# Moving the early half of an expert scatter ahead of a branch, and weight splits to other places, in a two-block transformer kernel

## The chip, the core and the metric

The kernel runs on one core of one Trainium2 chip. The metric is the device time of one execution in microseconds (us): the median of several runs, each timed from the start of the program to its end.

## What is computed

The input is 256 tokens of 1024 features, in float32, and a second sequence of 256 memory tokens. Two blocks of two layers each follow one another. Cut to what matters here:

```
first block, layer 0:  x += gate * (concat(retention(h), chunk_attention(h)) @ even_w_out)
             layer 1:  x += gate * (stick_breaking(h) @ odd_w_out)
  after each of them:  x += gate * grouped_moe(h)
second block, layer 0: x += norm(fox_and_nsa(h) @ ev_w_out)
              layer 1: x += norm(differential(h) @ od_w_out)
  after each of them:  x += norm(softmax((h @ wq) k_mem^T / 8) v_mem @ wo)   # 4 heads of 64
                       x += norm((silu(h @ wg) * (h @ wu)) @ wd)             # swiglu, 2816 wide
```

`grouped_moe` has 16 experts in 4 groups. Each token picks one group and two experts in it. The modulation of the first block (`gate`, and the scales and shifts inside `h`) comes from a matrix `ada_w` that is applied to one conditioning vector.

## The kernel before

**Products.** A float32 product is made of three TensorE products of rounded parts: each operand is the sum of a high part and a low part, and the low-by-low product is left out (`products`, L815 to L817; in the swiglu L1710 and L1711). A feature that PE turns into a bank goes to ScalarE (ACT), which writes the high part, and then to VectorE (DVE), which subtracts it for the low part.

**Weights.** SP's queue loads weights into a ring of three tiles of 1 MB, each in two halves of 512 KB. ACT copies a half to its high part (L1801, the helper `splits`), DVE subtracts for the low part (L2445, its own `splits`), and PE multiplies. DVE's subtraction is also what frees the half of the ring for SP's next load (L632). Both split buffers hold three tiles: ACT splits tile s only after PE has used tile s-3. The order of splits on ACT and DVE relative to their other work is written out by hand: a call `splits(end)` goes on with whole tiles up to a number, and waits if the load has not landed.

**Experts.** `experts(l)` runs a loop of four passes. Pass p computes, for the p-th expert of each group, up to a fixed number of gathered tokens. Tokens beyond that number are handled by an overflow body behind `If(over == 1)`; with these inputs the body is not taken, and each engine jumps over it. After the branch, `scatter` adds each pass's rows back to their tokens, with 32 matmuls for each layer (L1272 and L1273): 12 for the first three passes and the first two column parts, which need only the passes before the last (`early`), and 20 more which need the last pass's output too (`late`).

**Attention a0.** The first layer's chunk attention takes its pairs of heads in steps t. In each step, ACT writes exponentials and copies turned probabilities (L2000) and outputs (L2004, features of the output projection); DVE subtracts row maxima, scales, and writes the low part of the output features (L2755). Slices of the `ada` product are woven in on PE. `HIGH_AHEAD` and `LOW_AHEAD` name the steps at which ACT and DVE split whole tiles of `even_w_out`. PE then waits for all attention features before it starts `project("even_out")`, whose first tile multiplies features of the retention alone.

**Memory cross attention.** `cross(l)` on ACT: take 8 features (`take_features`), split weight tiles (the third of them, called f0 here, is the first of the swiglu that follows, and the next is f1), take the memory's projection (`take_mem`), copy the projected queries (L1854, `take_chunks`), split f1, and run the attention with its exponentials. The table of the exponential is loaded on ACT at the first of them, and `warm(ACT.Sqrt)` loads the root's table after the attention (L1874). DVE splits all these tiles ahead of its part of the attention (`shift`, L2717). After the attention comes the output projection, whose squares (L1879) ACT makes and whose norm DVE applies.

**End of the first swiglu.** The state is turned in 16 units of 128 features by 128 tokens (PE L930, ACT `take_state` L1838, DVE `low_state` L2676), which PE fills with products of the next projection `od_in`. Two calls `add_rows` on DVE add the normed rows to x (L2634). ACT then makes squares of x and splits the first tile of `od_in`'s second column group; DVE follows.

Of the kernel before, what the change touches and what calls it, by code (L numbers as in the profile page):

```python
# [15 lines left out]
KD = D // 128  # L16
# [10 lines left out]
RING = 3  # L27
# [167 lines left out]
def build(nc, a, out):  # L195
# [3 lines left out]
    with ctx:  # L199
# [244 lines left out]
        HIGH_AHEAD, LOW_AHEAD = {"a0": (4, 5), "b0": ()}, {"a0": (4, 6), "b0": ()}  # L444
# [348 lines left out]
        def _(eng):  # L793
# [470 lines left out]
            def scatter(m, l, high, taken, sources):  # L1264
# [12 lines left out]
                early, late = sources[:-1], sources[-1:]  # L1277
                if early:
                    eng.wait_ge(m["y_taken"], taken - 1)
                    for c in range(2):  # L1280
                        add_part(c, early, opens=True)
# [64 lines left out]
            def experts(l):  # L1346
# [21 lines left out]
                with eng.If(over == 1):  # L1368
                    def wait_over(i):
                        eng.wait_ge(ovf_loaded[l][i % RING], 16 * (i // RING + 1))  # L1370
                        return slot(i), slot(i)
                    eng.wait_ge(moe["y_taken"], PASSES * (l + 1) + 1)
                    experts_pass(ovf[l], 0, 5 * l + 4, wait_over, True)
# [404 lines left out]
        def _(eng):  # L1778
# [11 lines left out]

            def splits(end):

                while at_split[0] < end:
                    s = at_split[0]
                    at_split[0] += 1
                    t = tiles[plan.splits[s]]
                    for i in range(2):
                        eng.wait_ge(w_loaded[t["slot"]][i], t["loaded"])
                        if s >= SPLITS and i == 0:
                            eng.wait_ge(weights_used, tiles[plan.splits[s - SPLITS]]["order"] + 1)  # L1800
                        eng.activation(half_of(high(s), i, t["size"]), half_of(slot(t["n"]), i, t["size"]), ACT.Copy)\  # L1801
                           .then_inc(high_ready, 1)
# [1863 lines left out]
```

## Time and profile before

| what | us |
|---|---|
| median of 3 runs | 1750.7 |
| lowest and highest of the 3 | 1748.95, 1750.95 |
| the profiled execution's own time | 1750.65 |
| span of the profiled execution | 1748.9 |
| TensorE busy in that span | 1657.4 |

The profile shows one execution. PE is TensorE, DVE VectorE, ACT ScalarE, POOL GpSimd, SP the engine that issues the loads. Every instruction has its start, its duration, and the idle time of its engine before it, with what ended that idle time in square brackets. PEclk is the granted clock of TensorE as a share of full speed: 1.00 is 2.4 GHz, 0.50 is 1.2 GHz. Matmuls are pipelined, so that the distance between two starts tells more than one duration.

### The profile page before, as it was taken

The numbers are of one execution on the slowest core, as the hardware profiler recorded it, in microseconds if no ns is written. First come the engines' busy times: TensorE is split into PE (matmuls) and PEld (weight loads), VectorE is DVE, ScalarE is ACT, GpSimd is POOL, SyncE is SP. The second block draws the span as 40 slices with busy tenths as digits, with TensorE's granted clock in tenths as the row PEclk, the third lists the DMA queues.
The fourth block names the chain that finished last, engine by engine and source line by source line (L and its number), as shares of the span: only waits on it lengthen the run. The fifth ranks groups of instructions, "written<-read, shape, count | busy, mean of one in ns | idle before, by whom it ended". The sixth has DMA issues, their size and how long they took to land.

```text
span 1748.9 us, 24863 instructions
## 1 busy us (share of the span) xinstructions
PE 1657.4 (95%) x8427; PEld 1338.7 (77%) x8427; DVE 1278.9 (73%) x2067; ACT 1096.5 (63%) x1693; POOL 13.1 (1%) x27
## 2 busy tenths in 40 slices
PE   5998999999989999999999898889999898989998
PEld 3775778888878768888888787678888676868886
DVE  3874598988977586989989766676666657666665
ACT  3545488888864464888888675665444647654443
POOL 1000000000000000000000000000000000000000
PEclk8999899999999998999999999999999999989999
DMA  9878489999977563999999663116555551325552
GB/s 357 314 270 331 181 322 322 388 331 347 369 273 257 200 216 122 338 327 383 329 339 379 213 217 145 49 73 217 191 170 199 176 193 49 144 88 183 188 192 72
DMA packets 113345, 413.36 MB, mean 236 GB/s; under 512 B 13024, under 2 KB 13072, under 8 KB 112880
## 3 DMA queue, kind: packets, MB, share of 16 engines
q1 hardware_dynamic: 110208, 400.74, 63.3%
q0 software_dynamic: 1936, 8.59, 1.5%
q10 hardware_dynamic: 1120, 2.99, 0.4%
q8 instruction: 47, 0.77, 0.2%
q14 instruction: 34, 0.28, 0.0%
HBM read 411.21 MB, written 1.05 MB: 236 GB/s over the span
## 4 chain that ended last, share of the span: by engine, by line
PE 75%; DVE 10%; ACT 7%; issue 4%; DMA 3%; DVEq 0%; SPq 0%; ACTq 0%
PE banks L815 16%; PE banks L817 15%; PE banks L816 15%; PE banks L1710 10%; PE banks L1711 5%; DVE weights_low L2445 4%; PE banks L1033 1%; ACT qk_features L2050 1%; PE banks L992 1%; PE banks L832 1%; DMA weight_ring<-in_ada_w 1%; PE banks L845 1%; ACT weights_high L2142 1%; ACT scratch L1988 1%; ACT weights_high L1801 1%
## 5 line engine op out<-in xcount | busy, mean ns | idle before, releaser
L2445 DVE TENSOR_TENSOR weights_low<-weight_ring,weights_high 128x1024 fp32r<-128x1024 f32 (+1 forms) x656 | 770.7, 1218 | 142.6 <-ACT weights_high L1801 81.6
L815 PE MATMUL banks<-weights_high,features_parts 128*128 128x512 f32 (+1 forms) x1488 | 593.0, 399 | 16.0 <-DVE weights_low L2445 7.0
L817 PE MATMUL banks<-weights_high,features_parts 128*128 128x512 f32 (+1 forms) x1488 | 581.0, 390 | 0.0
L816 PE MATMUL banks<-weights_low,features_parts 128*128 128x512 f32 (+1 forms) x1488 | 580.6, 390 | 0.0
L2142 ACT ACTIVATE weights_high<-weight_ring 128x1024 fp32r<-128x1024 f32 x384 | 394.4, 1060 | 81.4 <-PE banks L817 51.4
L815 PEld LDWEIGHTS banks<-weights_high,features_parts 128*128 128x128 f32 x1488 | 281.1, 189 | 84.5 <-issue 12.4
L817 PEld LDWEIGHTS banks<-weights_high,features_parts 128*128 128x128 f32 x1488 | 280.8, 189 | 60.0
L816 PEld LDWEIGHTS banks<-weights_low,features_parts 128*128 128x128 f32 x1488 | 281.2, 189 | 54.7 <-issue 0.7
L1801 ACT ACTIVATE weights_high<-weight_ring 128x1024 fp32r<-128x1024 f32 (+1 forms) x176 | 176.7, 1044 | 122.6 <-PE banks L817 42.5
L1710 PE MATMUL banks<-features_parts,weights_high 128*128 128x512 f32 x704 | 252.7, 402 | 0.8 <-DVE features_parts L2580 0.8
L1711 PE MATMUL banks<-features_parts,weights_low 128*128 128x256 f32 x704 | 198.6, 282 | 0.0
L1710 PEld LDWEIGHTS banks<-features_parts,weights_high 128*128 128x128 f32 x704 | 133.4, 189 | 33.5 <-issue 1.1
L1711 PEld LDWEIGHTS banks<-features_parts,weights_low 128*128 128x128 f32 x704 | 134.0, 190 | 0.7
L2381 ACT ACTIVATE weights_high<-weight_ring 128x1024 fp32r<-128x1024 f32 x96 | 95.9, 1046 | 41.7 <-PE banks L1711 41.7
L2820 DVE SCALAR_TENSOR_TENSOR row_gains<-weight_ring,c_features,row_gains 128x512 f32<-128x512 f32 x84 | 63.1, 751 | 4.4
L3419 DVE TENSOR_REDUCE projected<-banks 128x256 f32<-128x512 f32 x44 | 30.3, 688 | 44.7 <-PE banks L1711 44.0
L2350 ACT ACTIVATE projected<-projected 128x256 f32<-128x256 f32 x44 | 18.4, 418 | 70.1 <-DVE projected L3409 70.1
L2357 ACT ACTIVATE features_parts<-projected 128x512 fp32r<-128x512 f32 x22 | 13.9, 630 | 68.3 <-PE banks L817 68.3
L3425 DVE TENSOR_TENSOR features_parts<-projected,features_parts 128x512 fp32r<-128x512 f32 x22 | 15.2, 692 | 43.0 <-ACT features_parts L2357 43.0
L3409 DVE TENSOR_REDUCE projected<-banks 128x256 f32<-128x512 f32 x44 | 30.1, 687 | 19.9 <-PE banks L1711 19.9
L1988 ACT ACTIVATE scratch<-scratch,row_shifts 128x128 f32<-128x128 f32 (+1 forms) x80 | 36.2, 454 | 9.1 <-DVE row_shifts L2717 9.1
L832 PE MATMUL banks<-fill 128*128 128x512 f32 x119 | 34.9, 433 | 0.3 <-DVE modulation L2838 0.3
(418 smaller groups left out, 1607.1 us busy)
## 6 DMA issues: line engine op xcount, KB each, us to landing
weight_ring<-in_exp_w_gate SPq DMA_DIRECT2D x128, 512.0 KB, 5.1
weight_ring<-in_exp_w_up SPq DMA_DIRECT2D x128, 512.0 KB, 5.0
weight_ring<-in_exp_w_down SPq DMA_DIRECT2D x128, 512.0 KB, 5.2
weight_ring<-in_ada_w SPq DMA_DIRECT2D x84, 512.0 KB, 5.5
weight_ring<-in_ffn_wg SPq DMA_DIRECT2D x44, 512.0 KB, 4.1
weight_ring<-in_ffn_wu SPq DMA_DIRECT2D x44, 512.0 KB, 4.5
weight_ring<-in_ffn_wd SPq DMA_DIRECT2D x44, 512.0 KB, 4.1
weight_ring<-in_even_w_in SPq DMA_DIRECT2D x28, 512.0 KB, 5.5
```

The source lines that it names most:

```text
L815: eng.matmul(dst, lh, rh, start=first, stop=False, **kw)
L816: eng.matmul(dst, lh, rl, start=False, stop=False, **kw)
L817: mm = eng.matmul(dst, ll, rh, start=False, stop=last, **kw)
L832: eng.matmul(B[bank][:, :], FILL[:, :], FILL[:, :].unsqueeze(1).to_broadcast([128, 4, 128]), start=True, stop=True, skip_group_check=True)
L1710: eng.matmul(both, wh, HHL[:, k], start=k == 0, stop=False, skip_group_check=True)
L1711: mm = eng.matmul(both[:, 0, :], wl, HH[:, k, :], start=False, stop=k == KD - 1, skip_group_check=True)
L1801: eng.activation(half_of(high(s), i, t["size"]), half_of(slot(t["n"]), i, t["size"]), ACT.Copy)\
L1988: eng.activation(p, p, ACT.Exp, scale=-1.0, bias=small(SHIFT, t)[:, i:i + 1], accum_out=small(SUMS, t)[:, i:i + 1]).then_inc(probs_ready, 1)
L2142: eng.activation(half_of(high(t["split"]), x), half_of(slot(t["n"]), x), ACT.Copy)\
L2381: eng.activation(half_of(high(t["split"]), x), half_of(slot(t["n"]), x), ACT.Copy)\
L2445: V(half_of(low(s), i, size), half_of(slot(n), i, size), half_of(high(s), i, size).bitcast(F32), ALU.subtract)\
L2820: ins = eng.scalar_tensor_tensor(out=acc, in0=w, scalar=CF[:, k:k + 1], in1=acc, op0=ALU.mult, op1=ALU.add)
```

## The change

Five places change.

1. `scatter` runs its 12 early matmuls and then calls `between`, which holds the branch; the body of the branch repeats the 12 at its end (`again`).
2. In attention a0 the splits of `even_out`'s first tile are made in halves: on ACT at t = 3 and 4, on DVE at t = 4 and 5. The second tile is split after the attention. PE's wait for the attention features moves behind the first tile of `even_out`.
3. In `cross(l)` the exponential's table is loaded right after the features are taken, and ACT copies the queries before it splits f0. ACT splits f0 in halves, one before and one after the attention. DVE splits f0 after its part of the attention. The root's table is loaded at step t = 2 of the attention.
4. In `feed_forward(l)` f1 is split between features 0 to 3 and 4 to 7.
5. At the end of the first swiglu both halves of the first tile of `od_in`'s second column group are split among the 16 units, and DVE's second `add_rows` comes two units earlier.

```diff
@@ plan
-        HIGH_AHEAD, LOW_AHEAD = {"a0": (4, 5), "b0": ()}, {"a0": (4, 6), "b0": ()}
+        HIGH_AHEAD, LOW_AHEAD = {"a0": (), "b0": ()}, {"a0": (), "b0": ()}
@@ PE
-            def scatter(m, l, high, taken, sources):
+            def scatter(m, l, high, taken, sources, between=lambda again: None):
...
                 early, late = sources[:-1], sources[-1:]
+
+                def open_first():
+
+                    for c in range(2):
+                        add_part(c, early, opens=True)
+
                 if early:
                     eng.wait_ge(m["y_taken"], taken - 1)
-                    for c in range(2):
-                        add_part(c, early, opens=True)
+                    open_first()
+                between(open_first)
                 eng.wait_ge(m["y_high"], high)
...
-                with eng.If(over == 1):
...
-                    scatter(ovf[l], l, 1, 1, [(PASSES, PASSES)])
-                    eng.wait_ge(ovf[l]["added"], 4)
-                scatter(moe, l, PASSES * (l + 1), PASSES * (l + 1) + 1, [(i, i) for i in range(PASSES)])
+                def overflow(again):
+
+                    with eng.If(over == 1):
...
+                        scatter(ovf[l], l, 1, 1, [(PASSES, PASSES)])
+                        eng.wait_ge(ovf[l]["added"], 4)
+                        again()
+                scatter(moe, l, PASSES * (l + 1), PASSES * (l + 1) + 1, [(i, i) for i in range(PASSES)], overflow)
...
             eng.wait_ge(mod_taken, 13)
-            eng.wait_ge(out_split, PAIR_OUTS["a0"])
             def within_out(j):
                 if j == 0:
+                    eng.wait_ge(out_split, PAIR_OUTS["a0"])
                     ada_parts(14, 0)
                     shift_products(0)
@@ ACT
+            def split_half():
+
+                s, i = at_split[0], halves[0]
+                t = tiles[plan.splits[s]]
+                eng.wait_ge(w_loaded[t["slot"]][i], t["loaded"])
+                if s >= SPLITS and i == 0:
+                    eng.wait_ge(weights_used, tiles[plan.splits[s - SPLITS]]["order"] + 1)
+                eng.activation(half_of(high(s), i, t["size"]), half_of(slot(t["n"]), i, t["size"]), ACT.Copy)\
+                   .then_inc(high_ready, 1)
+                halves[0] = 1 - i
+                at_split[0] += i
...
                 if t == 3:
                     eng.wait_ge(ada_used, 2 * (STRIPS.index(IN_SPLITS[-1]) + 1))
+                if t in (3, 4):
+                    split_half()
...
             def cross(l):
-                take_features(KD, lambda k: GM[:, 5 + 3 * l, k:k + 1])
+                take_features(range(KD), lambda k: GM[:, 5 + 3 * l, k:k + 1])
+                warm(ACT.Exp)
                 s = tiles[st[f"caq{l}"][0]]["split"]
-                splits(s + 3)
+                splits(s + 2)
                 take_mem(1 + 2 * l, B[4 + mem_chunk(l) % 4].rearrange("p (a n) -> p a n", a=2))
                 take_chunks(st[f"caq{l}"][1], lambda i: QK[:, i, :])
-                splits(s + 4)
-                attention(Pairs(f"ca{l}"))
-                warm(ACT.Sqrt)
+                split_half()
+                attention(Pairs(f"ca{l}"), between=lambda t: warm(ACT.Sqrt) if t == 2 else None)
+                split_half()
...
             def feed_forward(l):
-                take_features(KD, lambda k: GM[:, 6 + 3 * l, k:k + 1], 4)
+                s, gain = tiles[st[f"caq{l}"][0]]["split"], lambda k: GM[:, 6 + 3 * l, k:k + 1]
+                take_features(range(0, 4), gain, 4)
+                splits(s + 4)
+                take_features(range(4, KD), gain, 4)
...
-                    take_state(gain, range(4, 16))
+                    take_state(gain, range(4, 8))
+                    split_half()
+                    take_state(gain, range(8, 11))
+                    split_half()
+                    take_state(gain, range(11, 16))
@@ DVE (its own split_half waits for high_ready and subtracts one half)
...
+                if t in (4, 5):
+                    split_half()
...
             def cross(l):
...
-                splits(s + 4)
+                splits(s + 2)
                 attention(Pairs(f"ca{l}"))
+                splits(s + 3)
...
             def feed_forward(l):
-                low_parts(KD, lambda k: GM[:, 6 + 3 * l, k:k + 1], 4)
-                splits(tiles[st[f"caq{l}"][0]]["split"] + 5)
+                low_parts(range(0, 4), gain, 4)
+                splits(s + 4)
+                low_parts(range(4, KD), gain, 4)
+                splits(s + 5)
...
-                    low_state(gain, range(4, 8))
+                    low_state(gain, range(4, 6))
                     add_rows(1, done)
-                    low_state(gain, range(8, 16))
+                    low_state(gain, range(6, 8))
+                    split_half()
+                    low_state(gain, range(8, 11))
+                    split_half()
+                    low_state(gain, range(11, 16))
```

## Rows read from the trace of the kernel before

**Rows 1.** The page: TensorE's busy line, and the median landing of ada's loads.

```profile
PE 1657.4 (95%) x8427; PEld 1338.7 (77%) x8427; DVE 1278.9 (73%) x2067; ACT 1096.5 (63%) x1693; POOL 13.1 (1%) x27
...
weight_ring<-in_ada_w SPq DMA_DIRECT2D x84, 512.0 KB, 5.5
```

**Rows 2.** Waits of TensorE, whole run: total us, times, longest us.

```profile
PE banks L1272 <- DVE aux_rounded L3024: 4.3, 1, 4.3
```

**Rows 3.** Timeline of PE at the expert loops: start, us, operation, idle before.

```profile
193.65 0.95 PE L1015 MATMUL banks<-constants,row_gains 128*128 128x1 f32 x8
...
437.25 0.39 PE L815 MATMUL banks<-weights_high,features_parts 128*128 128x512 f32 x1
...
514.05 0.79 PE L1272 MATMUL banks<-projected_rounded 128*128 128x512 f32 x1 [4.95 <-issue]
...
518.27 0.39 PE L1273 MATMUL banks<-aux_rounded,projected_rounded 128*128 128x512 f32 x1
```

**Rows 4.** Windows: us, busy of PE, PEld, DVE, ACT, POOL, PEclk, DMA share, GB/s.

```profile
517.40:523.00 5.60, 5.60 (x25) 4.59 (x25) 3.74 (x6) 1.06 (x2) 0.00 (x0) 0.99 0.14 56
...
989.60:995.00 5.40, 5.38 (x13) 4.22 (x14) 1.40 (x2) 0.38 (x2) 0.00 (x0) 0.50 0.50 140
...
170.90:176.20 5.30, 5.29 (x13) 4.14 (x14) 2.17 (x2) 0.41 (x1) 0.00 (x0) 0.51 0.97 359
1380.00:1384.00 4.00, 4.00 (x20) 3.20 (x21) 2.03 (x6) 1.83 (x5) 2.10 (x4) 1.00 0.40 143
1534.20:1538.70 4.50, 4.47 (x24) 2.72 (x24) 2.21 (x5) 0.98 (x2) 0.00 (x0) 0.62 0.00 2
```

**Rows 5.** Timeline around the end of attention a0: SP, ACT, DVE, PE.

```profile
158.68 5.12 SPq L632 DMA_DIRECT2D weight_ring<-in_even_w_out  x4
...
166.55 2.00 ACT L1801 ACTIVATE weights_high<-weight_ring 128x1024 fp32r<-128x1024 f32 x2
...
167.64 2.36 DVE L2445 TENSOR_TENSOR weights_low<-weight_ring,weights_high 128x1024 fp32r<-128x1024 f32 x2 [3.52 <-ACT weights_high L1801]
...
170.39 0.41 DVE L2755 TENSOR_TENSOR features_parts<-banks,features_parts 128x256 fp32r<-128x256 f32 x1
...
170.91 0.76 PE L815 MATMUL banks<-weights_high,features_parts 128*128 128x512 f32 x1 [2.61 <-DVE features_parts L2755]
```

**Rows 6.** Timeline of cross attention 0: PE, ACT, DVE.

```profile
1159.64 0.80 PE L1060 MATMUL banks<-mem_keys_values,qk_features 64*128 64x256 f32 x2 [3.30 <-ACT qk_features L1854]
...
1159.47 2.01 ACT L1801 ACTIVATE weights_high<-weight_ring 128x1024 fp32r<-128x1024 f32 x2
...
1171.88 1.28 ACT L1874 ACT_TABLE_LOAD   x1
1173.17 0.20 ACT L1874 ACTIVATE unused_results<-epsilon 128x1 f32<-128x1 f32 x1
...
1162.85 0.42 DVE L2717 CUSTOM_DVE_ANT_0 scratch<-banks,constants 128x256 f32<-128x256 f32 x1
...
1174.78 0.15 DVE L2593 TENSOR_SCALAR partial_variance<-square_sums 128x1 f32<-128x1 f32 x1 [2.47 <-ACT projected L1879]
```

**Rows 7.** Timeline of cross attention 1: DVE, PE.

```profile
1526.52 2.36 DVE L2445 TENSOR_TENSOR weights_low<-weight_ring,weights_high 128x1024 fp32r<-128x1024 f32 x2 [0.56 <-ACT weights_high L1801]
...
1532.43 0.44 PE L1076 MATMUL banks<-constants,scratch 128*128 128x128 f32 x2 [2.08 <-DVE scratch L2735]
```

**Rows 8.** Timeline of the way into od_in: PE, ACT.

```profile
1380.00 0.33 PE L930 MATMUL banks<-constants,x_state 128*128 128x128 f32 x1 [1.01 <-DVE x_state L2634]
...
1392.83 0.80 PE L815 MATMUL banks<-weights_high,features_parts 128*128 128x512 f32 x1 [4.12 <-DVE weights_low L2445]
...
1382.78 0.37 ACT L1838 ACTIVATE features_parts<-banks,feature_gains 128x128 fp32r<-128x128 f32 x1 [0.43 <-PE banks L930]
...
1389.32 3.90 ACT L1801 ACTIVATE weights_high<-weight_ring 128x1024 fp32r<-128x1024 f32 x4 [0.23 <-DVE reciprocal_root L2687]
```

**Rows 9.** Waits of SP's queue from 230 to 500 us.

```profile
SPq L632 <- DVE weights_low L2445: 181.8, 182, 3.6
```

More of the change, by code:

```diff
@@ L1789, in _ @@
             at_split, parts = [0], [0]
+            halves = [0]
+            def split_half():
[8 more added lines that the diff above has]
+                at_split[0] += i
             def splits(end):
                 while at_split[0] < end:
[L1794 to L1802, printed above, removed]
+                    split_half()
             def high_features(k, count, taken=None):
@@ L1839, in take_state, with take_features @@
                        .then_inc(features_high, 1)
-            def take_features(count, gain=lambda k: 1.0, first=0):
-                for k in range(count):
+            def take_features(steps, gain=lambda k: 1.0, first=0):
+                for k in steps:
                     features[0] += 1
@@ L2418, in _ @@
             differences()
-            take_features(KD, lambda k: AG[:, 2:3])
+            take_features(range(KD), lambda k: AG[:, 2:3])
             norm_project("od_out", 24)
@@ L2446, in low_half, with split_half @@
                     .then_inc(split_ready, 1)
+            halves = [0]
+            def split_half():
+                s, i = at_split[0], halves[0]
+                n = plan.splits[s]
+                eng.wait_ge(high_ready, 2 * s + i + 1)
+                low_half(s, n, i, tiles[n]["size"])
+                halves[0] = 1 - i
+                at_split[0] += i
             def splits(end):
                 while at_split[0] < end:
-                    s = at_split[0]
-                    at_split[0] += 1
-                    n = plan.splits[s]
-                    for i in range(2):
-                        eng.wait_ge(high_ready, 2 * s + i + 1)
-                        low_half(s, n, i, tiles[n]["size"])
+                    split_half()
             def low_features(k, count):
@@ L2570, in _, with low_parts @@
             taken = copied["dve"]
-            def low_parts(count, gain=None, first=0):
-                for k in range(count):
+            def low_parts(steps, gain=None, first=0):
+                for k in steps:
                     parts[0] += 1
@@ L3394, in feed_forward @@
             def feed_forward(l):
-                low_parts(KD, lambda k: GM[:, 6 + 3 * l, k:k + 1], 4)
-                splits(tiles[st[f"caq{l}"][0]]["split"] + 5)
+                s, gain = tiles[st[f"caq{l}"][0]]["split"], lambda k: GM[:, 6 + 3 * l, k:k + 1]
+                low_parts(range(0, 4), gain, 4)
+                splits(s + 4)
+                low_parts(range(4, KD), gain, 4)
+                splits(s + 5)
                 base, f0 = tiles[st[f"ffn{l}"]], FFN_STEPS * l
@@ L3507, in _ @@
                 ins.then_inc(b1_mixed, 1)
-            low_parts(KD, lambda k: AG[:, 2:3])
+            low_parts(range(KD), lambda k: AG[:, 2:3])
             add_normed_project("od_out", 0)
```

14 lines of the change are left out of this document (8 added, 6 removed).

## Prediction

> **What bounds the kernel now.** The page comes first: TensorE (PE) is busy for 1657.4 of 1748.9 us [rows 1]. DVE and ACT are far from full, so taking work from them gains nothing by itself. Time can only come out of the 91 us in which PE stands still, or out of the stretches in which its clock is low. The second view is the list of PE's waits [rows 2]: one of the five places of the change shows there as a single long wait, and the other places have one in their stretch of PE's timeline [rows 3, 5 to 8]. The third view is windows of the granted clock behind such waits [rows 4]. A full-width matmul starts every 0.224 us at the full clock, 2.4 GHz (25 in 5.60), and every 0.41 us at 1.2 GHz (13 in 5.30 and in 5.40). A run of some 12 matmuls at the low clock thus costs 12 x 0.2 = 2.4 us more. Such a run follows the waits of 2.61, 4.25 and 4.95 us; after one of 1.01 us the clock stayed at 1.00 [rows 4, 8]. So a wait that shrinks to about 1 us gives back its length and these 2.4 us as well; a wait that is only moved gives back neither.
>
> **Scatter ahead of the branch (PE, both expert layers).** Before, PE stood 4.95 us in front of the first early matmul in layer 0. The profile ends that wait by "issue", that is, by nothing that another engine did [rows 3]: this is the jump over the overflow body. Layer 1 has 4.3 us in the same place [rows 2]; the profile names DVE there, but the early matmuls need nothing that DVE still had to make, so I read the same jump. A loop's jump backwards shows no gap: the first matmul of the next pass carries no idle time [rows 3]. In the change the 12 early matmuls run at the full clock, 12 x 0.224 = 2.7 us, where PE stands now, and the jump comes after them. The jump does not shrink. If it can begin only when the last early matmul is done, nothing is hidden. If PE's sequencer runs ahead of the array, it begins after x us, x between 0 and 2.7. The nearest row for handing over instructions is eight one-column matmuls in 0.95 us, 0.12 each [rows 3]; 12 of them make x = 1.4, which I take. The low clock then falls on the late matmuls instead. In layer 1 it cost 2.4 before and does after: gain 2.7 - 1.4 = 1.3. In layer 0 the first eleven intervals took 518.27 - 514.05 = 4.22 us instead of 2.46, so it cost only 1.8 before [rows 3]; with 2.4 after, the gain is 0.7. I take 1.9 together, with bounds of 4.7 (x = 0 and the low clock as cheap as before) and -0.8. The repeated 12 in the body are not run.
>
> The Trainium skill ("TensorE: Matmul & The Clock Gate", the table at its head) gives a queue of 64 instructions in front of the array. By that the sequencer could be at the branch almost at once, as in the first rival below; no row here shows it.
>
> **Attention a0.** Before, ACT copied a whole tile of two halves (166.55, 2.00 us) ahead of the last output copy, DVE subtracted it (167.64, 2.36 us) ahead of the last low part (170.39), and PE waited 2.61 us for that [rows 5], to go on at half the clock [rows 4]. After, the first half is split one step earlier. SP issued the four halves of the two out-projection tiles from 158.68 on [rows 5]; with a landing of about 5.5 [rows 1] the first is there at 164.2, about when ACT can take it. So one half lies ahead of the last output copy where two lay, and ACT is at it 1 us earlier; DVE's second half ends at about 169.0, some 1 us after ACT's. PE's wait for the attention features also moves behind the first tile of 24 matmuls, which needs only the retention's features. PE starts when DVE has the second half, at about 169.1 instead of 170.91: 1.8 us, with a wait of 0.8 left, which I judge by the 1.01 to keep the clock: 2.4 more. What is queued behind the moved wait are the `ada` slices and the shift products; PE gets there after 24 x 0.224 = 5.4 us, at 174.5, and DVE's last low part is done by then (170.8 even before), so the wait costs nothing. The second tile's splits are no later than now. Sum 4.2; I take 4.0, with bounds of 4.4 and 1.0 (if the clock falls anyway and the load is late).
>
> **Memory cross attention, first.** PE's wait of 3.30 before the scores is put down to ACT's query copies, which stood behind f0's load and split [rows 6]. The queries were therefore ready at 1159.64 - 3.30 = 1156.34. With the copies ahead of f0, the scores can start half a microsecond after that, at 1156.8. DVE's row maximum, which started at 1162.85 behind the splits of f1 (ACT made them from 1159.47 on), can start some 0.9 behind the scores, at 1157.7: 5.1 us earlier. The exponential's table load, 1.28 us by the root's load at 1171.88, lies in front of the queries, where ACT waited for f0. The splits that are put off need cover. DVE's two halves (2.4 us) go into the 2.47 us in which DVE waits for the squares at 1174.78 [rows 6]; ACT's half (1.0) takes the place of the root's load (1.28), which goes into the attention. If that cover is gone, the output norm is late by up to 1 us. I take 4.8, with 0.3 for late fillers and for f1 between the features, bounds 3.5 (a unit of the swiglu that waits for f1) and 5.2.
>
> **Memory cross attention, second.** Here the weights were already loaded, and the splits cost what DVE takes: two halves (1526.52, 2.36) directly ahead of the row maximum [rows 7]. Without them it starts up to 2.4 us earlier, PE's wait of 2.08 at 1532.43 goes, and with it the low clock of the next 4.5 us, in which PE was granted 0.62 [rows 4]. At full clock that stretch would take 4.5 x 0.62 = 2.8, 1.7 less; I take 1.2 of it, as part of the stretch is waiting for DVE. Sum 3.6, bounds 2.0 and 4.2. SP's load into f0's slot is issued later, but the tile is needed only some passes of the ring later.
>
> **The way into od_in.** Before, PE stood 4.12 us at 1392.83 for the first tile of the second column group, because ACT's four copies (1389.32, 3.90) began only behind the squares of x, and there was 1.01 of waiting for `add_rows` at 1380.00 [rows 8]. In the 16 units ACT waits 0.43 of each 0.80 us [rows 8]. A half of 1 us needs two such gaps, so the unit behind it may be late by 0.2, and the halves are done at about 1383.5. PE then goes from the first column group into the second without a stop: 4.1, and the 12 matmuls at the low clock go too, 2.4; `add_rows` two units earlier takes the 0.9. The other tile of that group is split right behind the squares, one tile earlier than now, by about 1391.5; PE needs it 24 x 0.224 = 5.4 us behind its new start of 1387.8, at 1393.2. Sum 7.4, bounds 7.5 and 5.0 (it waits a little for that tile, at the low clock).
>
> **Sum.** 1.9 + 4.0 + 4.8 + 3.6 + 7.4 = 21.7 us. The profiled execution took 1750.65 us, its span 1748.9 with 1.75 around it; the median of the runs is 1750.7, so that the two can be taken as one. 1750.65 - 21.7 = 1729.0. All upper bounds make 4.7 + 4.4 + 5.2 + 4.2 + 7.5 = 26.0 (1724.7), all lower ones -0.8 + 1.0 + 3.5 + 2.0 + 5.0 = 10.7 (1739.9).
>
> **Rivals.** (1) *The jump is hidden behind the early matmuls*, x about 0.2: 1.2 us more in each layer, 1726.6. For it: the profile names no engine for the 4.95. Chance 0.1. (2) *Nothing is hidden*, x = 2.7: 1.3 less in each layer, 1731.6. Chance 0.15. (3) *Loads bound the expert stage*, and what is gained ahead of it (a0's 4.0 and layer 0's 0.7) is waited for again: 1733.7. For it: the DMA share of 0.97 at 170.90 [rows 4]. Against it: SP waited 181.8 us in 270 for DVE to free halves [rows 9], so the ring, not the loads, sets the pace there. Chance 0.12. (4) *A table load drains ACT.* The exponential's and the root's load would cost about 1 us more each, on the path in both cross attentions: 4 us less, 1733. Against it: ACT's next activation starts at 1173.17, right at the end of the load of 1.28 [rows 6]. Chance 0.08. The Trainium skill ("ScalarE: Activation LUTs", on what a table load costs) gives 1283 ns and a drain of about 1380 ns; the trace agrees with the first figure and shows no such drain behind the load at 1171.88. (5) *Slower: loop jumps start to miss.* The body that PE skips grows by 12 matmuls, and ACT's, DVE's and PE's programs shift. If PE's backward jumps, three in each of the two expert loops and of the two swiglu loops, came to cost what the skipped branch costs (4.95, and 2.4 of low clock), each would take 7.3 us: 12 of them 88 us, 1817. It decides from three such jumps on (21.7 / 7.3). Against it: they show no gap now, and the loop bodies are not changed [rows 3]. Chance 0.03.
>
> **How the numbers follow.** My forecast as summed has 0.52, and the rivals 0.48 in their order. A measurement of this kernel can tell about 0.2%, 3.5 us, from no change. The forecast and the first four rivals are faster by more than that, and so are all lower bounds taken together; the last rival is slower (0.03). Of the forecast's 0.52 I leave 0.02 for no change and 0.02 for slower, where several places miss their lower bounds: faster 0.93, same 0.02, slower 0.05. The range reaches from all upper bounds together less the 1.75 by which the lowest of the three runs lies under their median, 1723, to all lower bounds together, 1740; it holds the first four rivals.
>
> **What would show it.** Right: the early L1272 matmuls directly behind the last products of the expert loop, then a wait of 3.5 to 5 us in front of the late ones (its length, plus the early ones' 2.7, gives x); at the start of `even_out` a wait under 1 us and the clock near 1; in the first cross attention a wait of about 0.5 for the query copies instead of 3.30; in the second none of 2.08; no wait for the first tile of `od_in`'s second group. Wrong: a wait for L2445 at the start of f0's or f1's products, units of the 16 that take well over 0.80, a longer wait for the loads in the expert passes, or gaps at the first matmul of a pass.

## The result and the profile after

The changed kernel takes 1722.44 us in the median of four runs (1720.39 to 1724.06), the kernel before 1750.83 in four runs beside it. The ratio is 0.9839, with an interval from 0.9822 to 0.9856: 28.4 us faster. The forecast was 1729.0, that is 21.7 faster, and its range began at 1723, so the time lies 0.6 us below the range. The sign and most places were right; one term of the sum was far too small.

The page of the changed kernel has this busy line for TensorE, to be set beside [rows 1]; the span is 1718.6 us against 1748.9.

```profile
PE 1645.6 (96%) x8427; PEld 1331.3 (77%) x8427; DVE 1277.3 (74%) x2067; ACT 1096.5 (64%) x1695; POOL 13.2 (1%) x27
```

Of the 30.3 us between the two spans, PE stood still for 18.5 less, and its busy time fell by 11.8. Its instructions are the same in number, and the granted clock rose from 0.978 to 0.986 in the mean over the span, so I put the second part down to the clock. The waits of PE over the whole run (total us, times, longest us) answer to [rows 2] and to the waits of [rows 3, 6, 8]:

```profile
PE banks L845 <- DVE small L3366: 4.3, 1, 4.3
...
PE banks L815 <- DVE weights_low L2471: 2.3, 8, 0.5
...
PE banks L1272 <- issue: 1.4, 1, 1.4
...
PE banks L1060 <- ACT qk_features L1870: 0.9, 2, 0.5
```

The waits for the scatter, for the weights of `od_in` and for the query copies are gone or short. One wait is longer than before: L845, the compressed keys of the second block, is 4.3. It comes up again below. Before, it was 1.3:

```profile
PE banks L845 <- DVE small L3332: 1.3, 1, 1.3
```

To size each place, I measured the same stretch in both traces, from the end of one instruction to the start of another that comes at the same place of PE's program. Gains are worked out from the two profiled executions.

| stretch | before | changed | gain | forecast |
|---|---|---|---|---|
| a0: end of the last value product to 25th matmul of `even_out` | 11.68 | 7.27 | 4.4 | 4.0 |
| layer 0: end of DVE's last split to the first instruction behind the scatter | 14.07 | 9.18 | 4.9 | 0.7 |
| layer 1: the same | 15.21 | 9.05 | 6.2 | 1.3 |
| wait for the compressed keys | 1.34 | 4.26 | -2.9 | none |
| first cross attention: end of the query products to the output projection | 16.08 | 11.19 | 4.9 | 4.8 |
| first of the 16 units to 60 matmuls behind the last one | 32.50 | 24.86 | 7.6 | 7.4 |
| second cross attention, as the first | 14.83 | 11.20 | 3.6 | 3.6 |

The gains make 28.7. PE was also 1.7 us earlier at 160 us, ahead of anything that was changed (most of it loads of the first 40 us that landed earlier in this execution), and 28.7 + 1.7 = 30.4 is the 30.3 by which the spans differ, within 0.1. That it fits so closely is luck, since two differences outside the stretches cancel. Behind the wait for the compressed keys the clock fell in the changed kernel's execution, so that the next 60 matmuls took 10.68 us instead of 9.14. Behind the second cross attention the 300 matmuls from its output projection on took 61.0 instead of 62.7, by the clock too; in a second profile of the kernel before they took 59.9. Both columns are single executions: the profiled one of the changed kernel is the fastest of its four, and several stretches turn out below to differ between executions of one program.

The scatter is where forecast and chip part. PE's timeline shows the first early matmul and the first late one of each layer:

```profile
503.39 0.50 PE L1272 MATMUL banks<-projected_rounded 128*128 128x512 f32 x1
...
507.85 0.47 PE L1272 MATMUL banks<-projected_rounded 128*128 128x512 f32 x1 [1.44 <-issue]
...
974.42 0.50 PE L1272 MATMUL banks<-projected_rounded 128*128 128x512 f32 x1
...
977.99 0.47 PE L1272 MATMUL banks<-projected_rounded 128*128 128x512 f32 x1 [0.54 <-DVE aux_rounded L3056]
```

The early ones start without a wait, and the late ones follow 4.46 and 3.57 us after the first early one, with 1.44 and 0.54 of standing still in place of 4.95 [rows 3] and 4.25, which [rows 2] round to 4.3. The wait of layer 1 is no longer the jump's: DVE's low part of the last pass ends it. The windows behind these waits, and those of a0 and of the way into `od_in` (columns as in [rows 4]), show the full clock in each:

```profile
167.20:172.50 5.30, 5.30 (x24) 4.39 (x24) 2.56 (x3) 0.80 (x1) 0.00 (x0) 1.00 0.99 397
507.85:512.50 4.65, 4.65 (x20) 3.83 (x21) 4.54 (x8) 0.94 (x2) 0.00 (x0) 1.00 0.94 332
977.99:983.40 5.41, 5.28 (x24) 4.05 (x25) 5.19 (x8) 1.97 (x6) 0.00 (x0) 1.00 0.56 166
1361.40:1365.40 4.00, 4.00 (x21) 3.14 (x20) 3.45 (x8) 3.40 (x7) 2.11 (x4) 1.00 0.55 178
```

In this execution the other places went as forecast. These rows stand in the order of the forecast: a0 (ACT's first half, DVE's second, PE), the first cross attention (PE, ACT, DVE, DVE again), the second (PE), and the way into `od_in` (PE, ACT, PE).

```profile
162.71 1.05 ACT L1810 ACTIVATE weights_high<-weight_ring 128x1024 fp32r<-128x1024 f32 x1
...
165.87 1.23 DVE L2471 TENSOR_TENSOR weights_low<-weight_ring,weights_high 128x1024 fp32r<-128x1024 f32 x1 [0.44 <-ACT weights_high L1810]
...
167.19 0.47 PE L815 MATMUL banks<-weights_high,features_parts 128*128 128x512 f32 x1 [0.67 <-DVE modulation L2870]
...
1144.23 0.49 PE L1060 MATMUL banks<-mem_keys_values,qk_features 64*128 64x256 f32 x2 [0.47 <-ACT qk_features L1870]
...
1141.42 1.28 ACT L1890 ACT_TABLE_LOAD   x1
1142.71 0.20 ACT L1890 ACTIVATE unused_results<-epsilon 128x1 f32<-128x1 f32 x1
...
1145.40 0.42 DVE L2749 CUSTOM_DVE_ANT_0 scratch<-banks,constants 128x256 f32<-128x256 f32 x1 [3.48 <-PE banks L1060]
...
1154.79 2.35 DVE L2471 TENSOR_TENSOR weights_low<-weight_ring,weights_high 128x1024 fp32r<-128x1024 f32 x2
1157.33 0.15 DVE L2625 TENSOR_SCALAR partial_variance<-square_sums 128x1 f32<-128x1 f32 x1 [0.19 <-ACT projected L1895]
...
1505.21 0.44 PE L1076 MATMUL banks<-constants,scratch 128*128 128x128 f32 x2
...
1361.41 0.27 PE L930 MATMUL banks<-constants,x_state 128*128 128x128 f32 x1
...
1363.58 1.05 ACT L1810 ACTIVATE weights_high<-weight_ring 128x1024 fp32r<-128x1024 f32 x1
...
1369.97 0.39 PE L815 MATMUL banks<-weights_high,features_parts 128*128 128x512 f32 x1
```

In a0 PE waits 0.67 instead of 2.61; what ends this wait is DVE's small `modulation` step, which stands right behind the second half of the split. In the first cross attention the scores wait 0.47 instead of 3.30, the row maximum follows 1.2 behind, and the two f0 halves of DVE end just in front of the norm. In the second, the row that had waited 2.08 has no idle time in front of it. At `od_in` the first unit carries no wait, a half of the split lies between two units, and the first matmul of the second column group (1369.97) has no idle time in front of it.

### The profile page after: what moved, and what is told of

It is laid out like the page before. It is cut to its first block, busy times and chain, and to the rows that moved or that the text cites. A ratio compares the mean times of both kernels' runs of the same rounds, so it can differ in the third digit from the quotient of the medians.

```text
span 1718.6 us, 24866 instructions
## 1 busy us (share of the span) xinstructions
PE 1645.6 (96%) x8427; PEld 1331.3 (77%) x8427; DVE 1277.3 (74%) x2067; ACT 1096.5 (64%) x1695; POOL 13.2 (1%) x27
## 4 chain that ended last, share of the span: by engine, by line
PE 77%; DVE 10%; ACT 6%; issue 4%; DMA 2%; DVEq 0%; POOL 0%; SPq 0%; ACTq 0%
PE banks L815 16%; PE banks L817 16%; PE banks L816 16%; PE banks L1720 10%; PE banks L1721 5%; DVE weights_low L2471 4%; PE banks L1033 1%; ACT qk_features L2066 1%; PE banks L992 1%; DVE row_gains L2852 1%; PE banks L845 1%; DMA weight_ring<-in_ada_w 1%; PE banks L832 1%; ACT scratch L2004 1%; PE banks L1096 1%
## 5 line engine op out<-in xcount | busy, mean ns | idle before, releaser
L3457 DVE TENSOR_REDUCE projected<-banks 128x256 f32<-128x512 f32 x44 | 30.3, 688 | 42.6 <-PE banks L1721 41.6
L3463 DVE TENSOR_TENSOR features_parts<-projected,features_parts 128x512 fp32r<-128x512 f32 x22 | 15.2, 692 | 43.0 <-ACT features_parts L2379 43.0
```

## The experiments

Three theories were put against each other. Theory 1: the sequencer hands the early matmuls over and jumps while they run, and the short wait that is left does not cost the clock. Theory 2: the recorded sum, in which the jump starts 1.4 us late and a cold run follows. Theory 3: the surplus came from loads that landed early.

**One part alone, and all but that part.** In the first run only the scatter moves, and the other four places are as before. In the second everything but the scatter changes; this is its edit against the changed kernel:

```diff
+                between(open_first)
                 if early:
                     eng.wait_ge(m["y_taken"], taken - 1)
                     open_first()
-                between(open_first)
...
-                        again()
```

> Only the scatter moves ahead of the branch; the other four places are as before. Theory 1 (the branch's jump runs beside matmuls that were handed over already, and the short wait that is left does not cost the clock): the wait in front of the late matmuls is 0.5 to 1.5 us in each layer, the clock behind it stays near 1, and the gain is 5.0 + 5.8 = 10.8 us, 1740. Theory 2 (the recorded sum, x = 1.4 and a cold run behind it): waits of 3.5 and 2.9, clock 0.5 behind them, gain 1.9, 1748.9. Theory 3 (what was gained beyond the sum came from loads that happened to land early, not from the scatter): 1748.9 too, but with the waits of theory 1 absent.

> The changed kernel with the branch back in front of the early matmuls; all else as changed. Theory 1: 10.8 us are given back, 1733. Theories 2 and 3: 1.9 given back, 1724.3. In all of them a0 keeps its 4.0, the cross attentions 4.6 and 3.2, and the way into od_in 8.0, read from PE's starts at those places.

Measured: 1739.71 for the scatter alone, 10.6 less than the 1750.27 of before beside it (ratio 0.9928, 0.9903 to 0.9953), and 1731.62 without it, 18.7 less (0.9892, 0.9873 to 0.9911). Theories 2 and 3 wanted 1748.9 and 1724.3. The two gains add up to 29.2, within 1 us of the whole, 28.4. So the surplus is the scatter's, and the other four places are worth 18.7, where the forecast had 19.8.

PE's sequencer shows what the jump does. The view of one source line gives its two executions, one in each layer (shortest, median and longest duration in ns; first and last start), first before the change, then after it:

```profile
L1368 PEldq COMPARE_BRANCH  x2: 4261/4598/4934, 509.1 to 985.3; - x2
```

```profile
L1377 PEldq COMPARE_BRANCH  x2: 342/2290/4238, 503.4 to 974.5; - x2
```

DVE's split that releases the first early matmul of layer 0 in the changed kernel:

```profile
502.05 1.29 DVE L2983 TENSOR_TENSOR features_parts<-qk_features,features_parts 128x512 fp32r<-128x512 f32 x2
```

It ends at 502.05 + 1.29 = 503.34, and the branch starts at 503.4, 0.1 us later: handing over 12 matmuls delays it by next to nothing. The long duration is layer 0's: there the branch still takes 4.24, beside the early matmuls. In layer 1 it takes 0.34. The two runs above, in the same view:

```profile
L1377 PEldq COMPARE_BRANCH  x2: 342/2458/4574, 508.3 to 979.5; - x2
```

```profile
L1377 PEldq COMPARE_BRANCH  x2: 4406/4580/4754, 505.8 to 982.6; - x2
```

**The clock alone.** Twelve matmuls whose result nobody uses stand ahead of the branch, and the early ones stay behind it (shown against the run without the scatter's move):

```diff
+                if early:
+                    stay_busy(scatter_bank(l, 0), 12)
                 between(open_first)
```

> As the run without the scatter's move, but 12 matmuls whose result nobody uses stand ahead of the branch in each layer, so that PE is busy for 2.7 us while it would stand. No work is moved: what changes is only the clock behind the jump. Theory 1: the wait shrinks from 4.95 and 4.25 to about 2 and 1.5, the clock stays near 1, and the 1.8 and 2.4 us of the low clock are saved: 4.2 less than without the move, about 1729. Theory 2 (the jump begins 1.4 us late and its wait of 3.5 still costs the clock): 2 x 1.4 more than without the move, about 1736.

Measured: 1726.98 (0.9859, 0.9838 to 0.9881), 4.6 less than without the move, although PE has 24 matmuls more to do. The two layers differ. The first row is the wait in front of the early matmuls of layer 0; in layer 1 there was none. Then the windows of those matmuls:

```profile
513.49 0.63 PE L1272 MATMUL banks<-projected_rounded 128*128 128x512 f32 x1 [2.62 <-issue]
```

```profile
513.49:517.96 4.47, 4.47 (x13) 3.49 (x14) 0.06 (x1) 0.00 (x0) 0.00 (x0) 0.62 0.69 255
988.58:991.37 2.79, 2.79 (x14) 2.26 (x13) 2.78 (x3) 1.72 (x3) 0.00 (x0) 1.00 0.56 163
```

In layer 0 the jump took 5.5 us, a wait of 2.62 was left, and the clock fell behind it (0.62); this layer gained nothing (14.73 by the stretch of the table). In layer 1 the jump took 0.34, no wait was left, the clock stayed at 1.00, and the stretch took 11.10 instead of 15.21. So filling the wait can pay without moving any work, as theory 1 has it, but it did so in one layer of two. The run doesn't part the clock from the jump, since layer 1's jump became short as well.

**Half of the early matmuls ahead.** Only the first column part, 6 matmuls:

```diff
-                    for c in range(2):
-                        add_part(c, early, opens=True)
+                    add_part(0, early, opens=True)
...
                 between(open_first)
+                if early:
+                    add_part(1, early, opens=True)
```

> The changed kernel with only the first column part, 6 of the 12 early matmuls, ahead of the branch. Theory 1: 1.4 us of work hides in the jump, a wait of 3 us stays in each layer and the clock behind it falls as after the other waits over 2.6 us: against the changed kernel 2 x (1.3 + about 2.2) = 7 us are lost, 1729.5. If the clock is not what counts, only 2.7 are lost, 1725. Theory 2: next to nothing is lost, 1723 to 1724.

Measured: 1724.36 (0.9842, 0.9814 to 0.987). By the medians 1.9 are lost, but the runs spread over 8 us here. By the stretches of the profiled executions 12.70 - 9.18 = 3.5 and 11.23 - 9.05 = 2.2 are lost, 5.7 together; against the 10.5 that layer 0 takes in the mean of the changed kernel's profiles (below) it is 2.2 in each layer, 4.4. The waits, and the windows behind them:

```profile
511.09 0.50 PE L1272 MATMUL banks<-projected_rounded 128*128 128x512 f32 x1 [3.30 <-issue]
...
984.28 0.50 PE L1272 MATMUL banks<-projected_rounded 128*128 128x512 f32 x1 [2.67 <-issue]
```

```profile
511.09:514.35 3.26, 3.26 (x8) 2.54 (x9) 0.73 (x1) 0.00 (x0) 0.00 (x0) 0.56 0.94 305
984.28:986.50 2.22, 2.22 (x10) 1.83 (x11) 1.43 (x3) 0.34 (x2) 0.00 (x0) 1.00 0.64 198
```

The clock fell behind 3.30 and not behind 2.67. Theory 1 expected it to fall behind both, so this run was half a miss: a wait over 2.6 us does not always cost the clock.

**The changed kernel again, and more of it ahead.** The second run has a third column part ahead (18 matmuls):

> The changed kernel once more, as the yardstick on this chip for the next run. Theory 1 gives what it gave: 1722 to 1723. If the loads of the first 50 us and at 1045 us land as before the change, the wait of 4.3 us in front of the compressed keys is back at 1.3 and the profile lies 3 us lower or, where the first loads are later, at the same time.

> The changed kernel with the early matmuls of a third column part ahead of the branch too: 18 matmuls, 4.1 us, where 12 were. Theory 1: they fill what is left of the jump; the wait of 1.44 in layer 0 falls under 0.5, that of layer 1, which ends with DVE's low part of the last pass, under 0.3, and 1 to 1.5 us are gained against the changed kernel, 1721. If the jump begins only behind the last early matmul after all, the waits stay and nothing is gained.

```diff
-                    for c in range(2):
+                    for c in range(3):
                         add_part(c, early, opens=True)
...
-                for c in range(2):
+                for c in range(3):
                     add_part(c, late, opens=not early, closes=True)
-                add_part(2, sources, opens=True, closes=True)
```

Measured: 1721.45 for the changed kernel (0.9833, 0.9819 to 0.9846) and 1719.76 with 18 ahead (0.9823, 0.9809 to 0.9836). The intervals overlap, so the gain of 1 to 1.5 is not shown. With 18 ahead the waits were 1.25 and 0.33, not under 0.5 and 0.3, since the jump took 5.42 in layer 0 and 4.49 in layer 1 in this execution; the stretches were 9.03 and 8.84. Two windows of the repeated run are the surprise, the start of `even_out` and the late matmuls of layer 0:

```profile
169.10:174.40 5.30, 5.01 (x15) 4.01 (x16) 2.86 (x5) 1.12 (x2) 0.00 (x0) 0.68 1.02 400
510.36:516.00 5.64, 5.64 (x18) 4.50 (x19) 4.43 (x7) 1.45 (x3) 0.00 (x0) 0.70 0.73 269
```

The clock fell behind the 0.67 of a0 and behind a wait of 1.81 in layer 0 this time, in the program that had kept it in both places (behind 0.67 and 1.44). So the second half of theory 1, that the short wait does not cost the clock, holds in some executions only.

**The pieces of a0 and of the cross attentions.** The first run puts PE's wait for the attention features back ahead of `even_out`; the second puts both table loads back:

> The changed kernel with PE's wait for the attention features back in front of the first out-projection tile; the splits stay in halves. In the changed kernel PE starts at 167.19 and DVE's last low part of the features ends at 167.49. If the halves carry the gain of a0, PE starts 0.3 later, the wait is 1.0 instead of 0.67, the clock stays near 1, and 3.7 of the 4.0 remain. If the moved wait carries it, the wait is above 2 and the clock falls: 3 us lost.

> The changed kernel with both table loads of the cross attentions where they were: the exponential's at the first exponential, the root's behind the attention. By the load's 1.28 and nothing behind it: the first exponential starts about 1 us later in each cross attention, the first square 0.2 to 0.5 later, 2.5 us in all. If a load also drains the engine for 1.4 us more, as the skill's figure has it, 2 us more in each cross attention: 6 to 7 in all.

```diff
             eng.wait_ge(mod_taken, 13)
+            eng.wait_ge(out_split, PAIR_OUTS["a0"])
...
-                    eng.wait_ge(out_split, PAIR_OUTS["a0"])
```

```diff
-                warm(ACT.Exp)
...
-                attention(Pairs(f"ca{l}"), between=lambda t: warm(ACT.Sqrt) if t == 2 else None)
+                attention(Pairs(f"ca{l}"))
                 split_half()
+                warm(ACT.Sqrt)
```

Measured in one execution each: 1720.42 and 1719.14. In a0 the wait was 1.08, the clock fell, and the stretch took 9.13; the executions with 0.67 whose clock fell as well had 8.9. So the moved wait is worth 0.2 at that clock, and the halves carry the rest; whether 1.08 loses the clock more often than 0.67 can't be told from one execution. With late tables each cross attention took 11.78 instead of 11.20 up to the output projection, 1.2 us in all. That is under both expectations: the exponential's load began even before DVE's first row maximum, so that the first exponential was 0.6 us late and not 1, and PE's output projection no later than that. So by these stretches the new places of the table loads are worth 1.2 of the 8.5 us.

**All early matmuls ahead, and the clock in a0.** Layer 0 has 24 ahead and layer 1 18; the second run also has three idle matmuls in the 0.67 of a0 (the last lines of the edit):

> The changed kernel with all 24 early matmuls of layer 0 (5.4 us) and 18 of layer 1 ahead of the branch. The jump took 4.5 to 5.7 us in the runs so far. Theory 1: the wait in front of the late matmuls of layer 0 falls under 0.4 however long the jump is, the clock never falls there, and the way from the end of DVE's split to the end of the scatter is 8.8 to 9.1 in both layers, where the changed kernel had 9.2 to 11.9 in layer 0: 1.5 us in the mean, 1720.

> As the run before, and three matmuls whose result nobody uses stand in the wait of 0.67 in front of the first out-projection tile in a0. In half of the executions with that wait the clock fell behind it (first 12 steps of 0.368 in place of 0.234, 1.6 us). Theory 1: the fillers keep the clock, the way to the 25th matmul is 7.3 to 7.5 in each execution, and 0.8 is gained in the mean: 1719. If the clock falls for another reason than this wait, the steps stay at 0.368 in about half of the executions.

```diff
-                    for c in range(2):
+                    for c in range(4 if l == 0 else 3):
                         add_part(c, early, opens=True)
...
-                for c in range(2):
+                for c in range(3):
                     add_part(c, late, opens=not early, closes=True)
-                add_part(2, sources, opens=True, closes=True)
...
-                    add_part(3, sources, opens=True, closes=True)
+                    add_part(3, late if early else sources, opens=not early, closes=True)
...
+            stay_busy(4 + st["even_out"][0][1][0] % 4, 3)
             eng.wait_ge(mod_taken, 13)
```

Measured: 1719.65 (0.9824, 0.981 to 0.9838) and 1721.10 (0.9828, 0.981 to 0.9845), neither clear of the changed kernel. The clock stayed up behind the late wait in both layers of both profiles, as expected. The expected wait under 0.4 did not come, and the stretches were 9.41 and 9.50, and 9.76 and 9.60 in the second run, not 8.8 to 9.1. In the first run, DVE's split that releases the early matmuls, PE's late ones of both layers, and the branch:

```profile
504.77 1.29 DVE L2982 TENSOR_TENSOR features_parts<-qk_features,features_parts 128x512 fp32r<-128x512 f32 x2
```

```profile
512.66 0.47 PE L1272 MATMUL banks<-projected_rounded 128*128 128x512 f32 x1 [0.75 <-issue]
...
982.76 0.47 PE L1272 MATMUL banks<-projected_rounded 128*128 128x512 f32 x1 [0.97 <-issue]
```

```profile
L1376 PEldq COMPARE_BRANCH  x2: 4872/4999/5126, 507.6 to 977.5; - x2
```

The split ends at 504.77 + 1.29 = 506.06, and the branch starts at 507.62 in layer 0: 24 matmuls with their 24 weight loads hold the sequencer back by 1.56, where 6, 12 and 18 held it by 0.07 to 0.14. Behind that lies a jump of 4.87. The second run shows the same 1.56. So handing over stops being free somewhere between 18 and 24 matmuls. The clock stayed up behind the fillers in a0 (7.27) in the one profile there is; as it did so in four of nine profiles without them, this shows little.

**Controls.** The kernel before once more, and the changed kernel with PE's code moved by 12 instructions:

> All five places undone: the kernel before, for a second profile of it. It tells what differs between two executions of one program: waits in front of the early scatter of 4 to 5.7 and 4.2 to 4.5, and the wait for the compressed keys, which was 1.3 before and 1.6 to 4.3 in the changed kernels. If that wait is 1.5 to 3 here too, it is not of the change; if it is 1.3 again, the change (or its earlier clock time) may lengthen it.

> The changed kernel with six more filler matmuls at the router of layer 1, far ahead of that layer's expert loop: PE's program behind them moves by 12 instructions, the scatter and its branch are untouched. In layer 1 the skipped branch took 0.34 in every kernel with exactly 12 matmuls ahead of it and 4.25 to 5.25 with none, 6 or 18. If the place of the code decides, the branch of layer 1 takes over 4 again, the wait in front of its late matmuls grows from 0.54 to about 1.3, and layer 0 is unchanged (4.2 to 5.4). If the 12 matmuls themselves decide, it stays at 0.34.

```diff
-                stay_busy(0, 0 if l == 0 else 5)
+                stay_busy(0, 0 if l == 0 else 11)
```

Measured: 1749.57 and 1720.92. The kernel before had jumps of 4.84 and 4.35 and waited 1.5 for the compressed keys. With the code moved, layer 1's branch took 0.34 as ever:

```profile
L1377 PEldq COMPARE_BRANCH  x2: 340/2792/5243, 505.0 to 977.3; - x2
```

So a shift by 12 instructions does not bring the long jump back; shifts of another size were not tried. In all seven profiles with exactly 12 matmuls ahead, early ones or fillers, layer 1's jump took 0.34, and in the seven with 0, 6 or 18 it took 4.25 to 5.25. Why, stays open.

**The wait for the compressed keys.** The DMA records of both kernels and of all twelve runs give, for the weight tile that these keys' stage splits, when the nearest load of instruction code started (counted from SP's issue of the tile's first half) and how long the second half took to land. Beside it stands how long PE waited:

```
code load starts after issue   profiles   landing of 2nd half   wait of PE
4.7 to 7.1 us                  4          4.3 to 4.8 us         1.3 to 1.8 us
0.3 to 1.0 us                  10         5.0 to 7.3 us         2.0 to 4.3 us
```

The four are the two of the kernel before, the one without the scatter's move, and the one with half of it. In the changed kernel ACT waits for that half:

```profile
1048.84 1.06 ACT L1810 ACTIVATE weights_high<-weight_ring 128x1024 fp32r<-128x1024 f32 x1 [2.97 <-DMA weight_ring<-in_ev_w_in]
```

A code load of 16 KB that used to come after this weight load now comes into it. That is a match in 14 profiles, not an experiment: that the code load delays the weights is not shown.

## Why the prediction missed

**Where PE stands.** Right: 28 us came out of 91 us of standing still and out of the low clock, and DVE's and ACT's busy times are as before (1277.3 for 1278.9, 1096.5 for 1096.5).

**Scatter.** This is the step that failed: "12 of them make x = 1.4, which I take" and "the low clock then falls on the late matmuls instead". Both halves were wrong. The branch starts 0.1 us after the release of the early matmuls, not 1.4. And the clock stayed up behind the wait that was left, 1.44 and 0.54 in the profiled execution, where I had charged 2.4 in each layer. With the branch at 0.1, the wait left is about 4.95 - 2.7 = 2.2 us. That lies between the 2.61 behind which the clock was low and the 1.01 behind which it was not, so the clock could come back as well, and I did not price that. A third premise, that the jump does not shrink, failed in layer 1, where it went from 4.26 to 0.34. So the term of 1.9 measured 11.1 here, and 10.6 as a change by itself. The sign that I had named, a wait of 3.5 to 5 us in front of the late matmuls, did not come.

Layer 1 is 2.7 hidden, some 2.6 of clock, and 0.7 because a jump of 0.34 leaves DVE to end the wait. Layer 0 is 2.7, 1.8 of clock and 0.5 of a shorter jump. Over the six profiles with the early twelve ahead of the branch, layer 0's stretch was 9.18 to 11.91, 10.5 in the mean, and layer 1's 9.04 to 9.19. Against 14.2 and 15.2, the means of the three profiles with the branch in front (the kernel before twice, and the run without the scatter's move), that is 3.7 and 6.2. The clock's part in layer 0 was luck in the profiled execution: it stayed up in three of these six (waits of 1.44, 1.79 and 1.93) and fell in three (1.81, 2.45 and 2.58). The bound of 4.7 was wrong for the same reason: it kept the low clock at both ends. It was also added up too low: with x = 0 and the low clock as cheap as before, each layer gains the whole 2.7, 5.4 together. The range would then have begun near 1722.2 and held the measured time, with the term still at half of what it measured.

**The rivals.** The first one, the hidden jump, was what happened, and its x of 0.2 was right; its price of 1.2 per layer kept my mistake with the clock. The Trainium skill ("TensorE: Matmul & The Clock Gate", the table at its head) gives the queue of 64 that spoke for it. The runs agree that it is deep, with the branch only 0.13 us behind the release of 18 matmuls and their weight loads. Behind 24 pairs, 48 instructions, which 64 would hold, the branch came 1.56 late; there the measurement decides. Loads did not swallow what was gained ahead of the experts: PE was 6.2 ahead at 176 us and still 5.7 at 503. No jump back of a loop began to miss. The table load drained nothing: the row at 1142.71 follows the load of 1.28 at once, and putting both loads back cost 1.2 us in both cross attentions together. The Trainium skill ("ScalarE: Activation LUTs", what a table load costs) has a drain of 1380 ns more, which no row here shows; the measurement decides.

**Attention a0.** Right, 4.4 for 4.0, in the executions in which the clock stays up. Of the nine profiles with the wait of 0.67, it stayed up in four and fell in five, where the stretch is 8.9 and the gain 2.8. The judgement "by the 1.01 to keep the clock" was too sure.

**Cross attentions and od_in.** Right: 4.9 for 4.8, 3.6 for 3.6, 7.6 for 7.4. The covers that I named held: DVE's late f0 halves end where the norm begins. The stretches of the changed kernel were 11.19 to 11.22 in both cross attentions of every profile with these moves but for the late tables. In the three profiles without them (the kernel before twice, and the scatter alone) they were 16.1 to 17.5 and 13.4 to 14.8, so that the exact agreement is luck in part: in the second, the wait of 2.08 to 2.18 lost the clock in two of the three, and where it did not the stretch was 13.4 and the gain would be 2.2.

**Not in the sum.** The wait for the compressed keys: 2.0 to 4.3 in the ten profiles of the second row above, against 1.3 and 1.5 in the kernel before, gives 0.5 to 2.9 back. In five of the ten the clock fell behind it as well, 1.5 more.

## What to carry to other kernels

An engine that stands in front of a jump can be given work ahead of it that the jump does not need: here the sequencer handed over up to 18 matmuls with their weight loads and jumped at once, so that the work ran beside the jump; 24 held the jump back. Price a TensorE wait that shrinks twice, with and without the clock behind it, and let the range hold both; and look at the branch itself in the trace, not only at the idle time behind it. A stage that comes earlier can also meet loads of code that it did not meet before; look for them when a wait grows.

## What the runs showed of the hardware

The skipped branch seems to wait for code. In each of the 21 long jumps a load of 16 KB of instructions starts 1.9 to 4.4 us after the end of DVE's split, and the matmul behind the jump follows 2.4 to 2.5 us behind that start, however long the jump. In the seven jumps of 0.34 such a load starts too, 1.9 to 2.1 us after the split, when the branch is long done, so the load alone does not make a jump long. No run changed the loads themselves. The DMA view of the jump in layer 0 of the kernel before lists it (packets, MB, share of 16 engines):

```profile
q8 instruction: 1, 0.02, 1.2%
```

The Trainium skill ("Runtime: NRT & Kernel Launch", instruction fetch mechanics) says that a taken branch whose target is outside the fetched window has to wait for a DMA fetch; the loads in the long jumps agree. In layer 0 the jump took 4.2 to 5.5 us over the 14 profiles.

The clock behind a short wait is not decided by the wait's length alone. It stayed at 1.00 behind 2.67 us in one place and fell to 0.68 behind 0.67 us in another, and the same program kept it in one execution and lost it in the next. What PE did before differs as well: the 0.67 follows eight matmuls of one column, the waits of the scatter follow full-width ones. No run sets the two apart. One such fall costs about 1.6 us (8.9 against 7.3 in a0). Two of them make 3.2 of the 3.7 us by which the first four runs of the changed kernel differ; that they are the reason is not shown, as one of the four is profiled.
